# Second attention: values as the stationary operand in two column tiles, the softmax division on GpSimd, the first scores inside the fills and the last pairs between the pieces of the output projection

## The reference, cut to what matters

```python
def axial_gqa_attention(h, w_qkv, q_gain, k_gain, w_o):
    qkv = h @ w_qkv
    ...
    q = apply_axial_rope(rmsnorm(q, q_gain), cos, sin) * (HEAD_DIM ** -0.5)
    k = apply_axial_rope(rmsnorm(k, k_gain), cos, sin)
    ...
    def attend_block(q_blk):
        scores = jnp.einsum('bkgqd,bksd->bkgqs', q_blk, kt).astype(jnp.float32)
        p = jax.nn.softmax(scores, axis=-1).astype(vt.dtype)
        return jnp.einsum('bkgqs,bksd->bkgqd', p, vt)
    o = lax.map(attend_block, qb)
    return o.transpose(1, 0, 4, 2, 3, 5).reshape(b, s, N_HEADS * HEAD_DIM) @ w_o
```

## Time and profile before

| | |
|---|---|
| Runs of the kernel before | 1320.66, 1320.84, 1321.23 us |
| Median | 1320.84 us |
| Profiled execution | 1320.79 us, span of the trace 1319.0 us |
| TensorE busy | 1296.9 us, 98% of the span |
| DVE, ACT, GpSimd busy | 915.6, 684.1, 98.8 us |
| HBM read | 232.54 MB |

### The profile page before, as it was taken

The page is one execution under the profiler, slowest core; times in us unless marked ns, Lnnn a source line. Parts: engine busy times, 40 slices in busy tenths (PEclk is TensorE's granted clock), DMA queues, the critical chain, the costliest instruction groups (busy, mean ns, idle before and its releaser), DMA issues.

```text
span 1319.0 us, 17782 instructions
## 1 busy us (share of the span) xinstructions
PE 1296.9 (98%) x7099; PEld 1115.7 (85%) x7105; DVE 915.6 (69%) x990; ACT 684.1 (52%) x819; POOL 98.8 (7%) x139
## 2 busy tenths in 40 slices
PE   9999999999999999999999999999999999999997
PEld 6868888888888888888888888888888888988886
DVE  5987755558567865556787664787777555677776
ACT  5664444445754444444656543566665543566663
POOL 3101000001330100000220100000001100000000
PEclk9999999999999999999999999999999999999999
DMA  9723655556443655554740633555557442455540
GB/s 343 301 96 128 205 192 191 191 191 229 160 158 104 248 191 191 191 191 166 253 175 14 223 129 129 203 189 190 189 188 252 160 160 93 162 185 189 190 170 32
DMA packets 36209, 235.56 MB, mean 179 GB/s; under 512 B 4152, under 2 KB 4528, under 8 KB 10160
## 3 DMA queue, kind: packets, MB, share of 16 engines
q1 hardware_dynamic: 30528, 217.07, 46.2%
q0 software_dynamic: 4608, 15.82, 3.7%
q10 hardware_dynamic: 1008, 1.77, 0.4%
HBM read 232.54 MB, written 2.10 MB: 178 GB/s over the span
## 4 chain that ended last, share of the span: by engine, by line
PE 85%; DVE 8%; ACT 3%; DMA 2%; issue 1%; POOL 0%; DVEq 0%; SPq 0%; POOLq 0%; ACTq 0%
PE ps L1928 22%; PE ps L1922 12%; PE ps L1943 7%; PE ps L1944 7%; PE ps L1945 7%; PE ps L1835 3%; PE ps L1805 3%; PE ps L1837 3%; PE ps L1806 3%; PE ps L1807 3%; PE ps L1836 3%; DVE wl L1069 2%; PE ps L2180 2%; PE ps L1775 1%; DMA raw<-in_w_slabs 1%
## 5 line engine op out<-in xcount | busy, mean ns | idle before, releaser
L1069 DVE TENSOR_TENSOR wl<-raw,wh 128x2048 fp32r<-128x2048 f32 x203 | 463.3, 2290 | 147.7 <-ACT wh L606 147.2
L606 ACT ACTIVATE wh<-raw 128x2048 fp32r<-128x2048 f32 x203 | 386.8, 1908 | 134.4 <-PE ps L1928 77.0
L1928 PE MATMUL ps<-xhl,wh 128*128 128x512 f32 x1376 | 328.2, 391 | 0.0
L1928 PEld LDWEIGHTS ps<-xhl,wh 128*128 128x128 f32 x1376 | 252.9, 188 | 48.9
L1922 PEld LDWEIGHTS ps<-xhl,wl 128*128 128x128 f32 x1376 | 176.1, 191 | 9.1 <-DVE wl L1069 1.6
L1922 PE MATMUL ps<-xhl,wl 128*128 128x256 f32 x1376 | 180.8, 284 | 1.3 <-DVE wl L1069 1.0
L1943 PE MATMUL ps<-wh,hh 128*128 128x512 f32 x432 | 168.3, 390 | 2.8 <-DVE hl L1362 2.8
L1944 PE MATMUL ps<-wl,hh 128*128 128x512 f32 x432 | 168.1, 389 | 0.0
L1945 PE MATMUL ps<-wh,hl 128*128 128x512 f32 x432 | 168.1, 389 | 0.0
L1943 PEld LDWEIGHTS ps<-wh,hh 128*128 128x128 f32 x432 | 81.1, 188 | 20.5 <-DVE hl L1362 3.7
L1945 PEld LDWEIGHTS ps<-wh,hl 128*128 128x128 f32 x432 | 81.1, 188 | 16.9
(11 more groups left out here) (278 smaller groups left out, 1700.7 us busy)
## 6 DMA issues: line engine op xcount, KB each, us to landing
raw<-in_w_slabs SPq DMA_DIRECT2D x203, 1024.0 KB, 4.8
raw<-in_w_slabs SPq DMA_DIRECT2D x4, 512.0 KB, 8.1
X<-in_x SPq DMA_DIRECT2D x2, 512.0 KB, 5.4
qk<-in_mem POOLq DMA_DIRECT2D x1, 1024.0 KB, 14.6
gains<-in_mem_norm POOLq DMA_DIRECT2D x2, 512.0 KB, 10.9
gains<-in_ln_mix_g POOLq DMA_DIRECT2D x2, 512.0 KB, 13.6
gains<-in_ln_mix_b POOLq DMA_DIRECT2D x2, 512.0 KB, 6.3
gains<-in_ln_ffn_g POOLq DMA_DIRECT2D x2, 512.0 KB, 4.2
```

What stands on the lines that cost most here:

```text
L606: nc.scalar.activation(wh[:, s % RING, :], raw[:, s % LOWS, :], ACT.Copy).then_inc(wh_ready, 1)
L1069: nc.vector.tensor_tensor(wl[:, s % LOWS, :], raw[:, s % LOWS, :], wh[:, s % RING, :].bitcast(F32), ALU.subtract)\
L1928: ins = nc.tensor.matmul(ps[bank + a], wa[:, kt, a * P:(a + 1) * P], xhl[:, kt, :, :], start=False, stop=(kt == KT - 1), skip_group_check= ...
```

## The change

TensorE. `values` for these pairs is replaced by `values_q(k)`, which serves two pairs, k and k + 1: the values of a key head (128 keys x 64 channels) are the stationary operand and the transposed probabilities of its four query heads (512 columns) the moving one; the two key heads write partitions 0 to 63 and 64 to 127 of one bank. The result is already transposed (channels by queries), so `prep` of TensorE for "wo" goes and ACT and DVE read banks 6 and 7 directly. The rows of `attn_w_o` are permuted on the host (`paired`) to fit that order. `scores_q(0)` moves into the first fill, `scores_q(1)` into the second, the transposes of queries stand ahead of the first fill and between the fills. Values of pairs 4 and 6 and transposes of pairs 6 and 7 move between the first four pieces of the output projection (`last_pairs`).

GpSimd. It multiplies the exps of a pair with the reciprocals of their sums in place, before TensorE transposes them; it waits for `q_sums`, TensorE for `p_norm`.

DVE. The reciprocal is made for each pair (`turn_q`), behind the maxima of the next pair and ahead of the copy of the pair before (`copy_q`). `qk_heads` goes. `query_scales("qk_q0")` stands earlier. The first evacuation for "wo" stands behind `copy_q(4)`, the last copy, `copy_q(7)`, ahead of the split of the projection's last slab.

ACT. `fill_out("F")` and a slab's high part stand behind the first exps, the first evacuation for "wo" behind the exps of pair 5.

The other users of `softmax`, `attention`, `values` and `project_out` keep what they did (the last output projection calls `between` at the same place as before). Two semaphore counts of the cross-attention are less by the eight pairs that no longer count there. The diff, cut to its core:

```diff
-    return half if pairs in ("wo", "hy_out") and t == 0 else base + t + 2 * half
+    if pairs == "wo":
+        return 6 + half
+    return half if pairs == "hy_out" and t == 0 else base + t + 2 * half
...
+    for k, (_, t, j) in enumerate(QK_PAIRS):
+        p = ar(QK_P, 2, 4, T)[:, k % 2]
+        pool.wait_ge(q_sums, k + 1)
+        nc.gpsimd.tensor_tensor(p, p, rr[:, t, 4 * j:4 * j + 4].unsqueeze(2).to_broadcast([P, 4, T]), ALU.mult).then_inc(p_norm, 1)
...
-    fill_out("F")
     splits(st["fillF"], 0, 1)
-    blocks(8, QK_FILLS, 4, (4,))
-    softmax(QK_PAIRS, Q_QK, None, lambda k: fill_out("F", 1) if k == 0 else None)
-    prep("wo", ts=(0,))
-    splits(st["fillF"], 1, 2)
+
+    def exps_q(k):
+        _, t, j = QK_PAIRS[k]
+        q = Q_QK + k
+        act.wait_ge(nb_ready, q + 1)
+        if k >= 2:
+            act.wait_ge(pT_ready, q - 1)
+        sc = score_bank("gqa", k % 2, T)
+        for u in range(4):
+            h = 4 * j + u
+            ins = nc.scalar.activation(ar(QK_P, 2, 4, T)[:, k % 2, u, :], sc[:, u // 2, u % 2, :], ACT.Exp, bias=nb[:, t, h:h + 1],
+                                       scale=qsc[:, t, 0, h:h + 1], accum_out=rs[:, t, h:h + 1])
+        ins.then_inc(exp_done, 1)
+
+    for k in range(len(QK_PAIRS)):
+        exps_q(k)
+        if k == 0:
+            fill_out("F")
+            blocks(8, QK_FILLS, 4, (4,))
+            splits(st["fillF"], 1, 2)
+        if k == 1:
+            fill_out("F", 1)
+        if k == 5:
+            prep("wo", ts=(0,))
...
+    def most_q(k):
+        _, t, j = QK_PAIRS[k]
+        dve.wait_ge(scores_ready, Q_QK + k + 1)
+        most = mx[:, t, 4 * j:4 * j + 4]
+        step(nc.vector.tensor_reduce(most.rearrange("p (j u) -> p j u", u=2), score_bank("gqa", k % 2, T), AX, ALU.max))
         sync()
-
-    def after_first():
-        blocks(8, QK_FILLS, 4, (5,))
-        query_scales("qk_q1", 8)
-
-    query_scales("qk_q0", 0)
+        nc.vector.tensor_tensor(nb[:, t, 4 * j:4 * j + 4], most, qsc[:, t, 1, 4 * j:4 * j + 4], ALU.mult).then_inc(nb_ready, 1)
+
+    def turn_q(k):
+        _, t, j = QK_PAIRS[k]
+        dve.wait_ge(exp_done, Q_QK + k + 1)
+        nc.vector.reciprocal(rr[:, t, 4 * j:4 * j + 4], rs[:, t, 4 * j:4 * j + 4]).then_inc(q_sums, 1)
+
+    def copy_q(k):
+        dve.wait_ge(pT_ready, Q_QK + k + 1)
+        if k >= 2:
+            dve.wait_ge(tr_done, 4 * PREPS.index("wo") + k // 2)
+        nc.vector.tensor_copy(gqa_pT(k), pall[:, 4:6, :].rearrange("p b s -> p (b s)")).then_inc(q_copied, 1)
+
+    most_q(0)
     splits(st["fillF"], 0, 1)
-
-    def qk_heads(t, c):
-        dve.wait_ge(pv_done, Q_QK + 4 * t + 2 * c + 2)
-        step(nc.vector.reciprocal(rr[:, t, 8 * c:8 * c + 8], rs[:, t, 8 * c:8 * c + 8]))
-        sync()
-        heads_out(xn[:, t, c * CH:(c + 1) * CH], ps[out_bank("gqa", t, 2 * c)][:, :], 8 * c, 8, 64, t).then_inc(xn_ready if c else half_out, 1)
-
-    softmax(QK_PAIRS, Q_QK, lambda k: qk_heads(k // 4, k % 4 // 2) if k in (1, 3, 5) else None, after_first)
-    prep("wo", ts=(0,))
+    turn_q(0)
+    blocks(8, QK_FILLS, 4, (5,))
+    query_scales("qk_q1", 8)
+    most_q(1)
     splits(st["fillF"], 1, 2)
+    for k in range(2, len(QK_PAIRS)):
+        most_q(k)
+        turn_q(k - 1)
+        copy_q(k - 2)
+        if k == 6:
+            prep("wo", ts=(0,))
+    turn_q(7)
+    copy_q(6)
+    copy_q(7)
...
+    def probs_q(k):
+
+        pe.wait_ge(p_norm, k + 1)
+        if k:
+            pe.wait_ge(q_copied, k)
+        p = ar(QK_P, 2, 4, T)[:, k % 2]
+        for u in range(4):
+            for b in range(TT):
+                c = u * T + b * P
+                ins = nc.tensor.transpose(ps[4 + c // CH][:, c % CH:c % CH + P], p[:, u, b * P:(b + 1) * P], ident)
+        ins.then_inc(pT_ready, 1)
+
+    def values_q(k, v):
+
+        _, t, j = QK_PAIRS[k]
+        pe.wait_ge(q_copied, k + 2)
+        if t:
+            pe.wait_ge(bank_free, st["wo"].f0 + 1 + j // 2)
+        for b in range(TT):
+            for a in range(2):
+                pT = gqa_pT(k + a).rearrange("p (u b s) -> p u b s", b=TT, s=P)[:, :, b, :]
+                o = ps[6 + j // 2][64 * a:64 * a + 64, :].rearrange("p (u s) -> p u s", s=P)
+                vc = 1280 + (j + a) * 64
+                ins = nc.tensor.matmul(o, v[:, b, vc:vc + 64], pT, start=(b == 0), stop=(b == TT - 1))
+        ins.then_inc(tr_done, 1)
...
-    fill("F")
-    qk_blocks(range(2, 4))
+    def scores_q(k):
+        if k >= 2:
+            pe.wait_ge(exp_done, Q_QK + k - 1)
+        scores(Q_QK + k, k % 2, *QK_PAIRS[k])
 
     def first_quad():
         pe.wait_ge(blk_act, 4 + 2)
         pe.wait_ge(blk_dve, 4 + 1)
-        scores(Q_QK, 0, *QK_PAIRS[0])
-        qk_blocks(range(4, 6), bank=4)
-
-    fill("F", 1, mid=first_quad)
+        scores_q(0)
+
+    def second_quad():
+        pe.wait_ge(blk_dve, 4 + 2)
+        scores_q(1)
+
+    qk_blocks(range(2, 4))
+    fill("F", mid=first_quad)
+    qk_blocks(range(4, 6), bank=4)
+    fill("F", 1, mid=second_quad)
     blocks_done(8, QK_FILLS)
-    attention(QK_PAIRS, Q_QK, nat, started=1, first_values=lambda: pe.wait_ge(fill_done, 8), before_last=lambda: prep(xn, xn_ready, xn_at("qk_heads"), ts=(0,), pairs="wo"))
-    project_out(st["wo"], xn, xn_ready, xn_at("qk_heads"), lambda: mem_prep(1), first=False)
+    scores_q(2)
+    probs_q(0)
+    scores_q(3)
+    probs_q(1)
+    scores_q(4)
+    pe.wait_ge(fill_done, 8)
+    values_q(0, nat)
+    probs_q(2)
+    scores_q(5)
+    probs_q(3)
+    scores_q(6)
+    values_q(2, nat)
+    probs_q(4)
+    scores_q(7)
+    probs_q(5)
+
+    def last_pairs(at):
+        if at == (0, 0, 0):
+            pe.wait_ge(exp_done, Q_QK + 7)
+        if at == (0, 0, 1):
+            values_q(4, nat)
+            probs_q(6)
+        if at == (0, 1, 0):
+            probs_q(7)
+        if at == (0, 1, 1):
+            values_q(6, nat)
+        if at == (1, 0, 1):
+            pe.wait_ge(bank_free, st["wo"].f0 + 4)
+            mem_prep(1)
+
+    project_out(st["wo"], None, None, None, last_pairs, first=False)
...
+    paired = a["attn_w_o"].reshape(2, 2, 4, 64, D).transpose(0, 2, 1, 3, 4).reshape(D, D)
...
-out += chunk(a["attn_w_o"], c * CH)
+out += chunk(paired, c * CH)
```

More of the change, by code:

```diff
@@ L705, in softmax @@
                         act.wait_ge(pT_ready, q - 1)
-                    for u in range(heads(kind)):
+                    for u in range(2):
                         sc = score_bank(kind, (q - q0) % ring(kind), w)
[L708 to L711, removed]
+                        ins = nc.scalar.activation(ar(pa, 2, 2, T)[:, q % 2, u, 0:w], sc[:, u, :], ACT.Exp,
+                                                   bias=nb[:, t, c + u:c + u + 1], accum_out=rs[:, t, c + u:c + u + 1])
                     ins.then_inc(exp_done, 1)
@@ L1822, in project_out @@
                         for half in range(2):
-                            if (t, c, half) == (0, 1, 1):
+                            if src is not None and (t, c, half) == (0, 1, 1):
                                 prep(src, w, v, ts=(1,))
-                            if between and (t, c, half) == (1, at_c, 1):
-                                between()
+                            if between:
+                                between((t, c, half))
                             s = stage.s0 + 2 * c + half
@@ L2139, in probs_T @@
                     pe.wait_ge(exp_done, q + 1)
[L2140 to L2144 removed]
+                for u in range(1 if kind == "diff" else 2):
                     for k in range(w // P):
                         c = u * w + k * P
[L2147 removed]
+                        o = ps[ring(kind) + q % 2][:, c:c + P]
                         ins = nc.tensor.transpose(o, p[:, u, k * P:(k + 1) * P], ident)
@@ L2152, in values @@
                 w = width(kind, t)
[L2153 removed]
+                pT = ar(pbuf(kind)[1], 2, CH)[:, q % 2]
                 copied[kind == "diff"] += 1
@@ L2160, in values @@
                     pe.wait_ge(bank_free, st[f"xq{int(q >= Q_XA[1])}"].f0 + 4 + 3 + t)
-                if kind == "gqa" and t and j == 0:
-                    pe.wait_ge(half_out, 1)
-                if kind == "gqa" and t and j == 2:
-                    pe.wait_ge(xn_ready, xn_count("qk_heads", 0))
                 bank = ps[out_bank(kind, t, j)]
-                for u in range(1 if kind == "diff" else heads(kind)):
-                    h = j if kind == "diff" else heads(kind) * j + u
+                for u in range(1 if kind == "diff" else 2):
+                    h = j if kind == "diff" else 2 * j + u
                     if mid and u == 1:
@@ L2386, in _ @@
                 else:
-                    project_out(st["xo1"], xn, xn_ready, xn_at("x_heads1"), first=False, at_c=1,
-                                between=lambda: prep(xn, xn_ready, xn_at("ffn1"), base=4, ts=(0,)))
+                    project_out(st["xo1"], xn, xn_ready, xn_at("x_heads1"), first=False,
```

(1 more changed line is left out.)

61 lines of the change are left out of this document (19 added, 42 removed).

## The result

The changed kernel took 1314.29 us (median of 5 runs, 1314.15 to 1316.52) against 1320.84 for the kernel before: a ratio of 0.995, 95% interval 0.994 to 0.996. Its profiled span is 1312.2 us against 1319.0. Run once more beside the later experiments it gave 1314.56 (1314.24 to 1315.38), so the time of a kernel comes back within 0.3 us.

The account below looks back on a forecast made before the run. TensorE was taken as the bound; removing 17.95 us (values, result's transposes, gaps) and adding 12.75 nets 5.2 us, from 1320.8 to 1315.6, stated as 1315.8 us; own range 1314.0 to 1317.8, overall range 1313.6 to 1320.2.

Parts of the forecast that it names:

- Values: Second attention on TensorE: eight values calls, 14.3 us, become four of 2.0 us, 8.0 us in all.
- rival A: Column halves of the values matmuls run in turn, 3.5 us a call: 1321.8 us, no change; chance 0.12.
- Multiplies: GpSimd's in-place division between exp and transposes: 2.05 us for each pair, bounds 1.9 to 4.1.
- Rival B: GpSimd's division is slower than taken; 3.6 us a multiply costs 3.5 us, giving 1319.3 us; chance 0.10.
- Gaps: TensorE's waits, the largest 2.0 us before transposes 1: 4.45 us added, 1.65 us of old gaps removed.
- Transposes, pieces and passages: TensorE: eight transposes 7.4 us, eight projection pieces 21.9 us; passages to another form add 0.3 us.
- Scores moved and pairs between pieces: Scores 0 and 1 go into the fills, whose work is unchanged; 2.74 us projection pieces cover the last pairs' chain.
- The second half of the projection: DVE's work needed for it is done by 727.1 us, TensorE gets there at 727.9: 0.8 us to spare.
- Rival C: GpSimd and DVE exclude each other for all DVE work; projection's second half 7.8 us late, 1323.6 us; chance 0.07.
- The nb product: DVE's 0.16 us product behind each reduce, said to come when GpSimd is done by this order.
- The clock in the 2.0 us gap: TensorE's clock might fall in the gap before transposes 1; not priced, it stood at 1.00 through earlier gaps.

Follow-up runs that it names:

- the run with one tile: Changed kernel with values_q loops exchanged and all values matmuls writing to the same half of the columns (column tile 0): 1321.44 us.
- the run without the division: Changed kernel without GpSimd's multiplication; transposes wait for the exps and the probabilities stay unnormalised: 1313.94 us.
- the run with the reciprocal first: Changed kernel with the reciprocal of pair 1 ahead of DVE's reduce of pair 2: 1314.66 us.

## Why the prediction was right, point by point

The sum was 5.2 us, the rewritten part gave 6.1, and the forecast 1315.8 was 1.5 us above the time, inside its own range of 1314.0 to 1317.8 but 0.3 us from its end. Of the span 0.9 us more went in the rewritten part than the sum had, which the points below add up, and 0.6 outside it: no term of the prediction stood for these, and that both parts of them went the same way is luck. What the forecast was made of is what happened: four calls of values of 1.87 us in place of eight of 1.8, the result's transposes gone from TensorE's rows, and the largest gap where it was expected.

- **Values.** 2.0 us a call was taken; 1.87 is measured, 0.5 us in all. The decision, that halves by column overlap as halves by row do, was right, though no row stood for it when it was taken; the run with one tile shows that it carried the forecast: it comes out within 0.4 us of rival A's time. The Trainium skill, TensorE: Matmul & The Clock Gate, Measured speedup vs the span model, which spoke against A, agrees in kind: two tiles of 64 columns gave 1.90 times here where its three tiles of 32 gave 2.38.
- **Multiplies.** 2.05 taken (bounds 1.9 to 4.1), 1.89 measured, just under the lower bound. Rival B's slacks ahead of transposes 1 to 6 were 0, 1.9, 0.95, 1.2, 0.9, 1.15; measured are 0, 1.9, 1.14, 1.07, 1.04 and 1.41. But its price was too low: for a doubled multiply (3.78) the gaps alone would give 4.0 by the changed kernel's distances, and 8.7 came, because the rival's sum had neither DVE's blocked instructions nor the clock.
- **Gaps.** 4.45 forecast, 3.2 measured (1.57, 0.41, 0.43, 0.34, 0.42 and none before the first piece). The place of the large one was right, its size 0.4 too large, as the multiply and DVE's steps before it were each taken a little long; the rest of the difference is in the last ones, 0.2 and 0.2, which did not come, and values 2 (0.65 for 0.34).
- **Transposes, pieces and passages.** Transposes were put at 0.93, as in the steady part before. The six ahead of the projection take 1.02 to 1.04 from start to start, the two between its pieces 0.85 and 0.79: 7.8 us where 7.4 had been put. The eight pieces take 22.6 where 21.9 had been put: the five that follow another form last 2.83 to 2.94, the other three 2.72, where 2.74 had been put for each. The prediction had 0.3 us for such passages; they came to 1.1, and 0.8 is missing in the sum. This is its largest omission besides the gaps, and of the opposite sign.
- **The sum once more.** Values -0.5, gaps -1.3, transposes and pieces +0.8, scores and mem_prep -0.1: the stretch is 1.15 us shorter than forecast (49.05 for 50.2). Ahead of scores 2 0.2 were lost on the forecast, so 0.9 remain.
- **Scores moved and pairs between pieces.** Taken at no cost, with their cover named. Both undone one by one cost 9.7 and 6.9 us. These covers are larger than the change's whole gain, and the prediction had no number for what they hold off, the clock above all.
- **The second half of the projection.** It had 0.8 us to spare by hand (727.1 against 727.9). DVE's first half of the evacuation ran from 725.02, 0.7 us of it, and the second half of the projection started without a gap: the whole chain was over 1 us earlier, and the margin stayed.
- **Rival C** did not come: reduces and copies took 1.19 to 1.23 us beside GpSimd. Of what the Trainium skill, SBUF — State Buffer, Who interferes with whom, says there, the prediction left out the half on instructions with one SBUF input that take both ports, and that half did bear, as the last section shows. The nb product was said in the prediction to come when GpSimd is done; that is so in the changed kernel, and the run with the reciprocal first shows what this sentence was worth, 0.68 us. What it overlooked is query_scales, which has one input in SBUF; it cost nothing in the changed kernel, where transposes 1 hang on reduce 2, and that on scores 2, as the run without the division shows.
- **The clock in the 2.0 us gap** stayed unpriced. The gap was 1.57 and the clock 1.00. In the profiled execution of the run in which DVE divides a gap of 2.01 left it at 1.00 as well; with 2.56, 3.97 and 3.98 it fell, and once with 1.77. So the forecast stood nearer to a step than its range admitted: with a multiply twice as long the change would have been no gain (1322.57).

Two things stay open. The 0.3 us upstream lie ahead of the changed instructions and are about what two profiles differ by in this place without a change ahead of it: in the runs above that leave scores 0 to 2 in their places scores 2 come 0.02 to 0.45 us later than in the changed kernel's first profile, once 1.0. Why TensorE waits 0.3 us less for a split far downstream was not tested.

## What to carry to other kernels

Two matmuls with 64 columns of weights each can be paired in the two halves of the columns at nearly the price of one (here with 128 rows and 512 moving columns, fp32); check such a change by a run that puts both into the same half. Before an elementwise step goes to GpSimd, list DVE's instructions in the time of that step by where their inputs lie: in these runs those that read PSUM passed, while the two small kinds that read only SBUF waited for its end, and one of 0.16 us ate a gain of 0.7. Other kinds were not met beside a multiply. An idle time on TensorE costs its length only while the clock holds behind it; where a change rests on cover (work put inside fills or between pieces), take into account that losing it costs the wait and then the half clock behind it.

## What the runs showed of the hardware that was not expected

- Small DVE instructions wait for the end of a GpSimd multiply: four of 128x8 with one SBUF input took 1.73 us instead of 0.39 beside one multiply, 3.43 beside two in a row, 0.38 once moved away and 0.38 at the old place with the multiplies left out; a 128x4 product took 0.84 instead of 0.16, and 0.16 with the multiply cut, and 1.57 in the kernel with doubled multiplies. A DVE subtraction with one input in PSUM and one in SBUF was not held up: two of 128x512 took 1.28 us at 714.36 beside a multiply of that kernel, as in the changed kernel at 708.45 without one. The Trainium skill, SBUF — State Buffer, Who interferes with whom, says this of both kinds (two SBUF inputs, and tensor_scalar where it takes both ports), and that whoever issues first holds the pair for its whole instruction; the trace agrees. Of the one-input kind the prediction had drawn only the lenient half.
- GpSimd's multiply was not lengthened: 1892 to 1894 ns for all eight, with reduces and copies out of PSUM on DVE beside it. No split of DVE met a multiply in this order; where one met a GpSimd product in the kernel before, that took 3.08 us instead of 1.04.
- The clock's fall differs between stalls of similar length. It fell with an idle time of 2.56 us (granted 0.57 in the 3.4 us behind it), 3.97 and 3.98, and not with 2.01; yet in the kernel with doubled multiplies it fell a second time (0.59 from 716.0 to 719.0) behind one of only 1.77, after 10.9 us in which TensorE had been busy for 7.8. It had fallen already while TensorE was idle only in the case of 3.98 (0.50 from 697.0 on); in the others it stood at 1.00 when TensorE came back and fell within a microsecond. In the kernel where DVE divides it was busy 10.67 of 15 us and the clock held. What separates these was not tried.
- In the column tiles the records of both heads start together whichever of the two loop orders issues them (1.87 and 1.88 us a call). Why the order doesn't matter stays open.
